# Reordering the token-major projections of a two-layer hybrid attention step, with their gates, rotations and inverse norms, its first loads and its end

## The chip, the core and the metric

The kernel runs on one core of a Trainium2 chip. The core has a matrix engine (TensorE, PE in the rows; PEld is its weight loads), VectorE (DVE), ScalarE (ACT), GpSimd (POOL) and a queue engine that issues most transfers (SyncE, SP). Each engine runs its own program in order; semaphores order work between engines. The metric is the device time of one execution: 3236.35 us, the median of three runs (3236.09 to 3236.82).

## The reference

Two post-norm layers over 128 context tokens and 512 latent tokens, width 1024. Each layer scales and shifts its input by a conditioning vector, projects it, mixes tokens in three head groups and projects back; then a dense feed-forward (first layer) or a top-2-of-8 expert feed-forward (second layer) follows, each with a residual and a layer norm.

```python
qa, ka, va, qkv_b, gate_b, a_b, b_b, qc, kc, vc = split_proj(h @ w_in_l)
oa = neighbourhood_attend(qa, ka, va, ...)
# gated DeltaNet, 4 heads, both directions
u = silu(short_conv(qkv, conv_w));  q, k, v = split(u, 3)
q = l2norm(q) * HEAD_DIM ** -0.5;   k = l2norm(k)          # x * rsqrt(sum(x*x) + 1e-6)
g = -exp(a_log) * softplus(a + dt_bias);  beta = sigmoid(b)
# differential attention: queries and keys of the latent tokens are rotated by their grid position
qc, kc = axial_rope(qc), axial_rope(kc)
x = layer_norm(ALPHA * x + g1 * (concat(oa, ob, oc) @ w_out))
x = layer_norm(ALPHA * x + g2 * channel_mixer(modulate(x)))
```

`a_b` and `b_b`, the decay and write gates, are 16 columns of the combined projection.

## The kernel before

The 640 tokens are five tiles of 128 (tile 0 is the context). A float32 product is done as three products of rounded words: a matrix is split in a rounded part ("high", cast by ScalarE) and the rest ("low", subtracted by VectorE), and high by high, high by low and low by high are summed. Weights come in loads of 1 MB through a ring of four slots; a load waits on `ring_used`, which TensorE counts up when it is done with a slot. All order is written by hand, in one program per engine (`build`, one block each).

**Start.** SyncE loads the conditioning, the constants and the five tiles of x (lines 617 to 622), then eight 1 MB blocks of the conditioning weights (line 628, from line 631). TensorE turns each block into six vectors per layer, block after block (`rows_of`, `columns_of`, lines 758 and 768), with ScalarE between (lines 1317, 1324). Then x is turned and modulated (lines 790 and 1743).

**Projections.** First 18 feature-major tiles (`FT`, line 819). Then 25 token-major groups n = 0 to 24 (`VT`, line 842): chunks c = 0 to 3 of 256 columns (values and output gates), five token tiles each, then c = 4, the 16 gate columns of five tiles. A group is 24 products, each with its own 128x128 weight load. VectorE empties the even groups (line 1801), ScalarE the odd ones (line 1368). Beside them VectorE runs six short convolutions (`convolve`, line 1786), one after each fourth group, and ScalarE their silu (line 1372).

**Between the projections and the DeltaNet.** After the last group, TensorE transposes the context keys for the output (line 852), multiplies the six rotated tiles by a permutation (line 858), sums squares of four tiles over each head (line 867), transposes keys and values (line 874) and sums the gates along time (lines 880, 882). GpSimd, VectorE: rotation (lines 2202, 1812, 1814). ScalarE: square, then log and exp for the inverse norm of one tile at a time (`square`, `inverse_norm`, lines 1387, 1394, 1397); VectorE multiplies by it (line 1828). ScalarE copies keys and values (line 1407), then softplus, exp of the gates (lines 1411 to 1419). Only then does the first of five DeltaNet units start (line 901).

**End.** The experts' rows are gathered by token (GpSimd, line 2180), scaled (ScalarE, line 1611), summed (VectorE, line 2140), multiplied by the gate row (GpSimd, line 2186); then residual and statistics of all five tiles (lines 2145, 2147), one inverse deviation for all (lines 1613, 1614), the two steps of the norm for all five (lines 2063, 2066), and five stores (lines 733, 735) behind one wait for all tiles.

## Time and profile before

| | |
|---|---|
| median of three runs | 3236.35 us |
| the profiled execution | 3239.69 us |
| its span in the trace | 3237.9 us |
| busy TensorE, VectorE, ScalarE, GpSimd | 2872.3, 1784.2, 1308.3, 338.0 us |
| share of the chain that ended last: TensorE, VectorE, ScalarE | 77%, 9%, 6% |

Times in rows are microseconds from the span's start unless marked ns. Of a row of the chain the columns are start, length, what. A matmul's length includes its way through the pipeline, so the spacing of starts, not the length, is what one of many costs. "Granted clock" is 1.00 for 2.4 GHz and 0.50 for 1.2 GHz. An idle time stands in brackets with what ended it.

### The profile page before, as it was taken

How to read it: one execution, taken by the hardware profiler on the slowest of the kernel's cores; microseconds unless marked ns; L12 is line 12 of the kernel's file. 1: busy time of each engine (PE TensorE's matmuls, PEld its weight loads, DVE VectorE, ACT ScalarE, POOL GpSimd, SP SyncE). 2: the span in 40 equal slices, each digit the busy share in tenths (PEclk: the TensorE clock that was granted, in tenths of full speed). 3: DMA queues.
4: the chain of work that ended last, by engine and by line, in shares of the span. 5: the costliest groups of instructions: out<-in, count | busy, mean ns of one | idle time of the engine just before them, and what ended most of it. 6: DMA issues, size and time to landing. Idle time of an engine off the chain costs nothing.

```text
span 3237.9 us, 51526 instructions
## 1 busy us (share of the span) xinstructions
PE 2872.3 (89%) x21532; PEld 2548.6 (79%) x21532; DVE 1784.2 (55%) x2706; ACT 1308.3 (40%) x1918; POOL 338.0 (10%) x335
## 2 busy tenths in 40 slices
PE   6997987897889999979979879988699999999992
PEld 5995776665889899769957766668589999899991
DVE  2243444667632222352524456666488888888886
ACT  2114222354132122131242224451477777777771
POOL 0002121100210000100021220002100000000002
PEclk9996988799999999979969888989899999999996
DMA  5251220000021221232221210003599999999992
GB/s 207 79 176 58 77 107 36 24 1 1 21 97 64 74 90 61 91 138 72 79 69 54 107 41 19 1 1 126 195 366 356 376 354 366 364 356 375 354 364 104
DMA packets 76518, 477.43 MB, mean 147 GB/s; under 512 B 10225, under 2 KB 13809, under 8 KB 26865
## 3 DMA queue, kind: packets, MB, share of 16 engines
q1 hardware_dynamic: 52672, 316.84, 26.1%
q0 software_dynamic: 23616, 157.30, 12.9%
q8 instruction: 173, 2.83, 0.3%
q14 instruction: 57, 0.46, 0.0%
HBM read 455.49 MB, written 27.53 MB: 149 GB/s over the span
## 4 chain that ended last, share of the span: by engine, by line
PE 77%; DVE 9%; ACT 6%; issue 4%; DMA 3%; POOL 1%; DVEq 0%; SPq 0%; ACTq 0%
PE psum L1258 14%; PE psum L1157 10%; PE psum L819 8%; PE psum L1280 7%; PE psum L842 5%; PE psum L1187 4%; PE psum L1118 4%; PE psum L1065 2%; DMA ring<-in_ada 2%; PE psum L931 2%; PE psum L1023 2%; PE psum L941 2%; ACT stage_rounded L1564 2%; PE psum L954 1%; PE psum L1050 1%
## 5 line engine op out<-in xcount | busy, mean ns | idle before, releaser
L1258 PE MATMUL psum<-stage_rounded 128*128 128x256 f32 x3728 | 571.6, 287 | 11.0 <-DVE ring_rounded L1633 4.3
L1258 PEld LDWEIGHTS psum<-stage_rounded 128*128 128x128 f32 x3728 | 512.7, 191 | 27.9 <-DVE ring_rounded L1633 11.8
L1633 DVE TENSOR_TENSOR ring_rounded<-ring,stage_rounded 128x2048 fp32r<-128x2048 f32 (+1 forms) x145 | 319.2, 2216 | 2.4 <-ACT stage_rounded L1564 2.4
L1633 DVE TENSOR_TENSOR stage_rounded<-stage,stage_rounded 128x2048 fp32r<-128x2048 f32 (+1 forms) x144 | 317.9, 2223 | 0.0
L1564 ACT CAST stage_rounded<-ring 128x2048 fp32r<-128x2048 f32 (+1 forms) x145 | 269.3, 1863 | 44.2 <-PE psum L1280 28.8
L1564 ACT CAST stage_rounded<-stage 128x2048 fp32r<-128x2048 f32 (+1 forms) x144 | 268.5, 1869 | 43.3 <-PE psum L1280 28.6
L1280 PE MATMUL psum<-stage_rounded 128*128 128x512 f32 x940 | 251.9, 394 | 0.1
L1459 ACT ACTIVATE stage<-psum,arena 128x640 f32<-128x640 f32 (+1 forms) x180 | 126.5, 706 | 231.5 <-DVE arena L1955 231.5
L1258 PE MATMUL psum<-ring_rounded,stage_rounded 128*128 128x256 f32 x760 | 215.3, 283 | 0.0
L1280 PEld LDWEIGHTS psum<-stage_rounded 128*128 128x128 f32 x940 | 175.1, 188 | 42.9 <-DVE stage_rounded L1633 3.7
L1065 PEld LDWEIGHTS psum<-stage 128*128 128x128 f32 x1008 | 135.0, 204 | 67.5 <-issue 35.7
L1065 PE MATMUL psum<-stage 128*128 128x128 f32 x1008 | 153.2, 299 | 29.3 <-ACT stage L1466 16.7
L1157 PE MATMUL psum<-stage_rounded 128*128 128x320 f32 x704 | 161.8, 311 | 12.0 <-POOL ring_rounded L2258 12.0
L1955 DVE TENSOR_REDUCE arena<-psum 128x1 f32<-128x640 f32 (+1 forms) x180 | 123.1, 712 | 73.9 <-PE psum L1026 38.2
L1157 PE MATMUL psum<-input_rounded,stage_rounded 128*128 128x320 f32 x704 | 161.5, 311 | 0.0
L1157 PE MATMUL psum<-stage_rounded,ring_rounded 128*128 128x320 f32 x704 | 161.1, 310 | 0.0
L1534 ACT CAST stage_rounded<-ring 128x2048 fp32r<-128x2048 f32 (+2 forms) x38 | 64.0, 1683 | 239.8 <-PE psum L1157 130.9
L1258 PEld LDWEIGHTS psum<-ring_rounded,stage_rounded 128*128 128x128 f32 x760 | 145.9, 192 | 0.3
L1435 ACT COPY stage<-psum 128x512 f32<-128x512 f32 x100 | 58.6, 586 | 210.5 <-PE psum L941 210.5
L1753 DVE TENSOR_TENSOR ring_rounded<-ring,stage_rounded 128x2048 fp32r<-128x2048 f32 x26 | 59.5, 2290 | 141.5 <-ACT stage_rounded L1344 141.5
L2117 DVE TENSOR_TENSOR stage<-stage,psum 128x640 f32<-128x640 f32 x22 | 18.1, 822 | 216.5 <-PE psum L1157 216.5
L1187 PE MATMUL psum<-stage_rounded 128*128 128x512 f32 x440 | 135.9, 389 | 0.0
(303 smaller groups left out, 6061.8 us busy)
## 6 DMA issues: line engine op xcount, KB each, us to landing
ring<-in_ada SPq DMA_DIRECT2D x48, 1024.0 KB, 4.9
ring<-in_moe_gu SPq DMA_DIRECT2D x48, 1024.0 KB, 7.3
ring<-in_moe_gu POOLq DMA_DIRECT2D x47, 1024.0 KB, 8.0
stage<-in_moe_gu SPq DMA_DIRECT2D x46, 1024.0 KB, 7.5
stage<-in_moe_gu POOLq DMA_DIRECT2D x46, 1024.0 KB, 7.6
ring<-in_unit SPq DMA_DIRECT2D x22, 1024.0 KB, 4.7
stage<-in_moe_down SPq DMA_DIRECT2D x22, 1024.0 KB, 7.4
stage<-in_moe_down POOLq DMA_DIRECT2D x22, 1024.0 KB, 7.8
```

The lines of the kernel that those rows point to most:

```text
L819: mm = pe.matmul(bank(b + g, 0, HALF), w[:, i % 2, k, :], r32(x[:, k, g * HALF:(g + 1) * HALF]), start=(k == 0 and m == 0), stop=(k == KD ...
L842: mm = pe.matmul(bank(b, 0, 256 if c < 4 else 16), r32(x[:, k, t * P:(t + 1) * P]), w[:, k, :], start=(k == 0 and m == 0), stop=(k == KD - ...
L1065: mm = pe.matmul(bank(7, 256, 256 + P), probT[j % 2][:, s * P:(s + 1) * P], VT[:, s, v_at:v_at + P], start=(s == 0), stop=(s == n - 1))
L1118: mm = pe.matmul(bank(n % 4, 0, 256), r32(x[:, k, t * P:(t + 1) * P]), w[:, k, :], start=(k == 0 and m == 0), stop=(k == KD - 1 and m == 2))
L1157: mm = pe.matmul(bank(b + 2 * i + g, 0, HALF), w[:, i, k, :], r32(x[:, k, g * HALF:(g + 1) * HALF]), start=(k == 0 and n == 0), stop=(k == ...
L1187: mm = pe.matmul(bank(b), r32(x[:, f, cols]), w[:, j, :], start=(f == 0 and m == 0), stop=(f == UF - 1 and m == 2))
L1258: mm = pe.matmul(bank(h % 2, 0, 2 * P), r32(x[:, cols]), w[:, k, :], start=(k == 0 and m == 0), stop=(k == KD - 1 and m == 2))
L1280: mm = pe.matmul(bank(4 + g), r32(x[:, f, :]), w[:, at], start=(f == 0 and m == 0), stop=(f == UF - 1 and m == 2))
L1459: act.activation(dst, src, ACT.Exp, bias=nb[:, s:s + 1], accum_out=sm[:, s:s + 1]).then_inc(a_exp, 1)
L1564: act.copy(r32(M_HIGH[q % M_HI][:, 0:n]), M_SLOT[q % M_SLOTS][:, 0:n]).then_inc(a_mhi, 1)
L1633: v.tensor_tensor(r32(w), w, high(M_HIGH[q % M_HI][:, 0:n]), ALU.subtract).then_inc(v_mlo, 1)
L1955: v.tensor_reduce(nb[:, s:s + 1], src, AX.XY if t else AX.X, ALU.max, negate=True).then_inc(v_nb, 1)
```

## The change

The 16 gate columns become the first five token-major groups (`TOKM_ORDER`), and their moving operand is repeated eight times, so that each of their 120 products has 128 columns (eight equal copies; only 16 are read). The gates' arithmetic on ScalarE and VectorE moves between the later groups (after n = 4, 7, 10, 16, 19 and 22), the gates' sums on TensorE after n = 13. The six rotation products follow groups 2, 6, 10, 14, 18, 22, all in PSUM bank 5, and VectorE's rotation follows every fourth group. Squares of three of the four tiles move into the loop. Behind the loop the sums of squares go in six pieces to six banks, ScalarE takes six logs and then two exps over two tiles each, the keys' first; the transposes wait for the keys alone. The silu of the output gates and the conditioning's silu come after the copies of keys and values. At the start the tiles of x are issued after the fourth conditioning block. At the end each tile's sum, residual, statistics, deviation, norm and store follow one another. The buffers of the moved values move with them: the rotation's product to `RL` with one buffer in place of two, the squares to the buffers that then hold the inverse norms.

```diff
+        SUM_BANKS = (4, 5, 1, 2, 3, 0)
+
+        def piece(p):
+            return (norm_k, norm_q)[p // 3][:, NORM_CUTS[p % 3]:NORM_CUTS[p % 3 + 1]]
...
-            for t in range(TILES):
-                sp.dma_start(xt[t], x_in[t * P:(t + 1) * P, :]).then_inc(s_x_in, 16)
...
                 for i in range(ADA_FIRST):
                     load(ada_in[l, i], i)
+                    if l == 0 and i == RING - 1:
+                        for t in range(TILES):
+                            sp.dma_start(xt[t], x_in[t * P:(t + 1) * P, :]).then_inc(s_x_in, 16)
...
-            sp.wait_ge(v_x2, mixed_before(DEPTH))
+            sp.wait_ge(v_x2, mixed_before(DEPTH - 1, 1))
             sp.dma_start(y_prompt, xt[0]).then_inc(s_y_out, 16)
             for t in range(1, TILES):
+                sp.wait_ge(v_x2, mixed_before(DEPTH - 1, t + 1))
                 sp.dma_start(y_sample[(t - 1) * P:t * P, :], xt[t]).then_inc(s_y_out, 16)
...
                 for n in range(25):
-                    c, t = n // TILES, n % TILES
+                    i, t = n // TILES, n % TILES
+                    c = TOKM_ORDER[i]
                     if t == 0:
-                        pe.wait_ge(v_pl, PROJ * l + FEAT_LOADS + c + 1)
+                        pe.wait_ge(v_pl, PROJ * l + FEAT_LOADS + i + 1)
...
-                            mm = pe.matmul(bank(b, 0, 256 if c < 4 else 16), r32(x[:, k, t * P:(t + 1) * P]), w[:, k, :],
+                            wk = w[:, k, :] if c < TOKM_LOADS else w[:, k, :].unsqueeze(1).broadcast_to([P, 8, 16])
+                            mm = pe.matmul(bank(b, 0, 256 if c < TOKM_LOADS else P), r32(x[:, k, t * P:(t + 1) * P]), wk,
                                            start=(k == 0 and m == 0), stop=(k == KD - 1 and m == 2))
-                            if k == 0 and t == 0 and m == 0:
+                            if k == 0 and t == 0 and m == 0 and i != 1:
                                 mm.then_inc(ring_used, 1)
...
+                    if n % 4 == 2:
+                        r = n // 4
+                        if r == 0:
+                            pe.wait_ge(s_rope, 16 * (l + 1))
+                        else:
+                            pe.wait_ge(v_rot, 12 * l + 2 * (r - 1) + 1)
+                        pe.matmul(bank(5), perm, FT[:, 12 + r, P:TOK], start=True, stop=True).then_inc(s_rot, 1)
...
+                        pe.wait_ge(v_g, l + 1)
...
+                        mm.then_inc(s_gc, 1)
...
+                def sum_squares(p):
+                    x = piece(p)
+                    pe.matmul(bank(SUM_BANKS[p], 0, x.shape[1]), blocks, x, start=True, stop=True).then_inc(s_ss, 1)
+
+                pe.wait_ge(a_sq, 4 * l + 3)
+                pe.wait_ge(v_gc, 2 * l + 1)
+                pe.wait_ge(v_rot, 12 * l + 11)
+                sum_squares(0)
+                sum_squares(1)
...
                 pe.wait_ge(a_tokm, 12 * l + 12)
                 for j, i in enumerate((3, 4, 5, 15, 16, 17)):
                     mm = pe.transpose(bank(6 + j // 4, (j % 4) * P, (j % 4 + 1) * P), FT[:, i, 0:P], ident)
+                    if j == 0:
+                        mm.then_inc(ring_used, 1)
                     if j in (3, 5):
                         mm.then_inc(s_kt, 1)
...
+                sum_squares(2)
+                pe.wait_ge(a_sq, 4 * l + 4)
+                for p in range(3, 6):
+                    sum_squares(p)
+
+                pe.wait_ge(v_norm, 4 * l + 2)
+                pe.wait_ge(a_silu, 6 * l + 6)
                 for t in range(TILES):
...
+                pe.wait_ge(a_kout, l + 1)
+                pe.wait_ge(v_kout, l + 1)
+                pe.wait_ge(v_norm, 4 * l + 4)
                 pe.wait_ge(a_kv, 5 * l + 5)
                 pe.wait_ge(v_gc, 2 * l + 2)
...
+                    if i == FEAT_TILES - 1:
+                        act.wait_ge(s_par, 16 * (l + 1))
+                        act.copy(r32(ab_hi), par[:, PR_WAB:PR_WAB + KD * 16]).then_inc(a_ph, 1)
                     projection_high(i // 2 + 1)
...
-                    if n in (1, 7, 11):
-                        projection_high(FEAT_LOADS + 1 + n // TILES)
-                    if n == 17:
-                        act.wait_ge(s_par, 16 * (l + 1))
-                        act.copy(r32(ab_hi), par[:, PR_WAB:PR_WAB + KD * 16]).then_inc(a_ph, 1)
+                    c, t = TOKM_ORDER[n // TILES], n % TILES
+                    if n in (1, 11, 17):
+                        projection_high(FEAT_LOADS + (1, 11, 17).index(n) + 1)
                     act.wait_ge(s_tokm, 25 * l + n + 1)
-                    w = 256 if c < 4 else 16
+                    w = 256 if c < TOKM_LOADS else 16
                     act.copy(VT[:, t, c * 256:c * 256 + w], bank([0, 1, 2, 3, 6, 7][n % 6], 0, w)).then_inc(a_tokm, 1)
...
+                        if i in (0, 2, 3):
+                            act.wait_ge(a_silu, 6 * l + i + 1)
+                            act.activation(norms[i], FT[:, 6 + i, :], ACT.Square).then_inc(a_sq, 1)
+                    if n == 7:
...
+                    if n == 19:
+                        act.wait_ge(v_gc, 2 * l + 2)
...
+                act.wait_ge(s_tokm, 25 * (l + 1))
+                act.activation(norms[1], FT[:, 7, :], ACT.Square).then_inc(a_sq, 1)
                 act.wait_ge(s_kt, 2 * l + 1)
+                act.copy(kout[:, 0:512], bank(6)).then_inc(a_kout, 1)
+
+                for p in range(6):
+                    x = piece(p)
+                    act.wait_ge(s_ss, 6 * l + p + 1)
+                    act.activation(x, bank(SUM_BANKS[p], 0, x.shape[1]), ACT.Ln, bias=RMS_EPS).then_inc(a_ln, 1)
+                act.wait_ge(a_ln, 6 * (l + 1))
+                for x in (norm_k, norm_q):
+                    act.activation(x, x, ACT.Exp, scale=-0.5).then_inc(a_rs, 1)
+
+                for t in range(TILES):
+                    act.wait_ge(s_kvt, 5 * l + t + 1)
+                    act.copy(KV[:, t, :], bank(t)).then_inc(a_kv, 1)
...
                 spread_cond()
-
                 act.wait_ge(v_tokm, 13 * l + 13)
                 act.wait_ge(a_tokm, 12 * l + 12)
                 act.activation(VT[:, :, 768:1024], VT[:, :, 768:1024], ACT.Silu).then_inc(a_gsil, 1)
...
+            def weigh(t):
                 act.wait_ge(s_gt[t], 32)
                 act.wait_ge(v_route, WEIGHED)
                 act.activation(YS[0][:, t, :], YS[0][:, t, :], ACT.Identity, scale=wts[:, 5 + t:6 + t]).then_inc(a_y, 1)
-            act.wait_ge(v_var, NORMS * DEPTH)
-            link(act.activation(rstd, mv.rearrange("p (t c) -> p t c", t=TILES)[:, :, 1], ACT.Ln, bias=LN_EPS))
-            act.activation(rstd, rstd, ACT.Exp, scale=-0.5).then_inc(a_rstd, 1)
+
+            def last_deviation(t):
+                act.wait_ge(v_var, NORMS * DEPTH - 1 + t + 1)
+                link(act.activation(rstd[:, t:t + 1], mv[:, 2 * t + 1:2 * t + 2], ACT.Ln, bias=LN_EPS))
+                act.activation(rstd[:, t:t + 1], rstd[:, t:t + 1], ACT.Exp, scale=-0.5).then_inc(a_rstd, 1)
+
+            for t in range(3):
+                weigh(t)
+            for t in range(TILES):
+                last_deviation(t)
+                if t + 3 < TILES:
+                    weigh(t + 3)
...
-                for n in range(0, 25, 2):
-                    c, t = n // TILES, n % TILES
-                    if n in (2, 6, 12):
-                        projection_low(FEAT_LOADS + 1 + n // TILES)
-                    if n == 18:
-                        v.wait_ge(a_ph, PROJ * (l + 1))
...
-                for r in range(6):
+                ab = VT[:, :, 1024:1040]
...
+                def rotate(r):
                     x = FT[:, 12 + r, P:TOK]
                     v.wait_ge(s_rot, 6 * l + r + 1)
                     v.wait_ge(g_rot, 6 * l + r + 1)
-                    v.tensor_tensor(x, bank(r), sinT, ALU.mult).then_inc(v_rot, 1)
+                    v.tensor_tensor(x, bank(5), sinT, ALU.mult).then_inc(v_rot, 1)
                     v.wait_ge(v_rot, 12 * l + 2 * r + 1)
-                    v.tensor_tensor(x, x, rot[:, (r % 2) * 512:(r % 2 + 1) * 512], ALU.add).then_inc(v_rot, 1)
-
...
+                for n in range(0, 25, 2):
+                    c, t = TOKM_ORDER[n // TILES], n % TILES
+                    if n in (2, 12, 18):
+                        projection_low(FEAT_LOADS + (2, 12, 18).index(n) + 1)
...
+                    if n == 4:
...
+                    if n % 4 == 0 and n < 24:
+                        convolve(n // 4)
+                    if n == 10:
+                        v.wait_ge(a_gate, 6 * l + 3)
...
+                    if n == 16:
+                        v.wait_ge(s_gc, l + 1)
+                        v.tensor_copy(gct, bank(4, 0, 80)).then_inc(v_gc, 1)
...
+                    if n == 22:
+                        v.wait_ge(a_gate, 6 * (l + 1))
...
+                    if n % 4 == 0 and n:
+                        rotate(n // 4 - 1)
+
+                v.wait_ge(s_kt, 2 * l + 2)
+                v.tensor_copy(kout[:, 512:768], bank(7, 0, 256)).then_inc(v_kout, 1)
...
+                for j in (2, 3, 0, 1):
                     x = FT[:, 6 + j, :]
-                    v.wait_ge(a_rs, 4 * l + j + 1)
-                    v.scalar_tensor_tensor(x, x, HD ** -0.5 if j < 2 else 1.0, norms[j % 2], ALU.mult, ALU.mult).then_inc(v_norm, 1)
...
+                    v.wait_ge(a_rs, 2 * l + (1 if j >= 2 else 2))
+                    v.scalar_tensor_tensor(x, x, HD ** -0.5 if j < 2 else 1.0, norms[j], ALU.mult, ALU.mult).then_inc(v_norm, 1)
...
+
+                    def residual(t):
+                        v.wait_ge(g_xg, TILES * l + t + 1)
+                        link(v.scalar_tensor_tensor(xt[t], xt[t], ALPHA, YS[1][:, t, :], ALU.mult, ALU.add))
+                        for i in range(2):
+                            link(v.bn_stats(st_m[:, 12 * t + 6 * i:12 * t + 6 * i + 6], xt[t][:, i * 512:(i + 1) * 512]))
+                        carry(v)
+                        v.bn_aggr(mv[:, 2 * t:2 * t + 2], st_m[:, 12 * t:12 * t + 12]).then_inc(v_var, 1)
+
+                    def last_norm(t):
+                        v.wait_ge(v_var, NORMS * DEPTH - 1 + t + 1)
+                        link(v.scalar_tensor_tensor(xt[t], xt[t], mv[:, 2 * t:2 * t + 1], ln_g, ALU.subtract, ALU.mult))
+                        v.wait_ge(a_rstd, NORMS * DEPTH - 1 + t + 1)
+                        v.scalar_tensor_tensor(xt[t], xt[t], rstd[:, t:t + 1], ln_b, ALU.mult, ALU.add).then_inc(v_x2, 1)
+
+                    combine_rows(0)
+                    combine_rows(1)
+                    residual(0)
+                    combine_rows(2)
+                    for t in range(1, TILES):
+                        residual(t)
+                        if t + 2 < TILES:
+                            combine_rows(t + 2)
+                        last_norm(t - 1)
+                    last_norm(TILES - 1)
...
-
-                pool.wait_ge(s_tokm, 25 * (l + 1))
                 for r in range(6):
                     i = 12 + r
                     pool.wait_ge(a_feat if i % 2 else v_feat, 9 * l + i // 2 + 1)
-                    if r >= 2:
-                        pool.wait_ge(v_rot, 12 * l + 2 * (r - 1))
-                    pool.tensor_tensor(rot[:, (r % 2) * 512:(r % 2 + 1) * 512], FT[:, i, P:TOK], cosT, ALU.mult).then_inc(g_rot, 1)
+                    if r:
+                        pool.wait_ge(v_rot, 12 * l + 2 * r)
+                    pool.tensor_tensor(rot, FT[:, i, P:TOK], cosT, ALU.mult).then_inc(g_rot, 1)
```

On TensorE, at the end of the token-major groups of the first layer, before:

```order
L842 MATMUL psum<-stage_rounded 128x16 x2
L842 MATMUL psum<-stage_rounded,input_rounded 128x16
L852 MATMUL psum<-arena,stage 128x128 x6
L858 MATMUL psum<-stage 128x512 x6
L867 MATMUL psum<-stage,arena 128x320 x8
L874 MATMUL psum<-arena,stage 128x128 x20
L880 MATMUL psum<-arena 128x20 x2
L882 MATMUL psum<-arena 128x20 x2
L901 MATMUL psum<-stage 128x128 x2
```

and at the same place of the changed program, where L858 is the token-major product, L880 a sum of squares, L891 the context keys, L905 keys and values and L926 the first DeltaNet unit:

```order
L858 MATMUL psum<-stage_rounded 128x256
L858 MATMUL psum<-stage_rounded,input_rounded 128x256
L880 MATMUL psum<-arena 128x512 x2
L891 MATMUL psum<-arena,stage 128x128 x6
L880 MATMUL psum<-arena 128x256
L880 MATMUL psum<-stage,arena 128x512 x2
L880 MATMUL psum<-stage,arena 128x256
L905 MATMUL psum<-arena,stage 128x128 x20
L926 MATMUL psum<-stage 128x128 x2
```

The 16-column groups, the six rotation products and the four gate sums are gone from this place (they stand earlier), and the eight sums of squares are six.

On ScalarE, in the same stretch, before (L1387 square, L1394 log, L1397 exp; ACT_TABLE_LOAD switches the function table):

```order
L1387 ACTIVATE stage<-stage 128x640 x2
L1394 ACT_TABLE_LOAD
L1394 ACTIVATE stage<-psum 128x640
L1397 ACT_TABLE_LOAD
L1397 ACTIVATE stage<-stage 128x640
L1387 ACTIVATE stage<-stage 128x640
```

a pattern that runs four times. In the changed program, from the last square to the copies of keys and values:

```order
L1416 ACTIVATE stage<-stage 128x640
L1418 COPY stage<-psum 128x512
L1423 ACT_TABLE_LOAD
L1423 ACTIVATE arena<-psum 128x512 x2
L1423 ACTIVATE arena<-psum 128x256
L1423 ACTIVATE stage<-psum 128x512 x2
L1423 ACTIVATE stage<-psum 128x256
L1426 ACT_TABLE_LOAD
L1426 ACTIVATE arena<-arena 128x1280
L1426 ACTIVATE stage<-stage 128x1280
L1430 COPY stage<-psum 128x512 x5
```

Eight table loads between the squares and the copies have become two.

On VectorE, at the very end, the changed program has for one tile after the other (L2181 residual, L2183 and L2185 statistics, L2176 sum of the next tile's rows, L2189 and L2191 norm of the tile before):

```order
L2181 SCALAR_TENSOR_TENSOR arena<-arena,stage 128x1024
L2183 BN_STATS stage<-arena 128x6 x2
L576 MEMSET arena 128x1
L2185 BN_AGGR arena<-stage 128x2
L2176 SCALAR_TENSOR_TENSOR stage<-stage,arena 128x1024
L2189 SCALAR_TENSOR_TENSOR arena<-arena 128x1024
L2191 SCALAR_TENSOR_TENSOR arena<-arena 128x1024
```

where before each of these steps ran over all five tiles before the next.

## Rows read from the trace of the kernel before

**Rows 1.** Windows: busy time by engine with counts, granted clock, DMA share, GB/s.

```profile
184.60:241.70 57.10, 57.05 (x480) 57.08 (x481) 33.89 (x59) 11.62 (x17) 0.00 (x0) 1.00 0.68 231
247.20:262.50 15.30, 15.27 (x73) 15.18 (x72) 2.38 (x6) 0.98 (x3) 0.00 (x0) 0.50 0.00 1
264.07:271.00 6.93, 6.93 (x13) 2.95 (x13) 5.01 (x7) 4.41 (x6) 3.59 (x3) 0.74 0.63 189
```

**Rows 2.** The chain that ended last, both layers: start, length, what.

```profile
184.65 77.83 PE psum L842 x600
264.28 6.89 PE psum L858 x12
288.51 0.84 DVE stage L1828
289.39 4.54 PE psum L874 x20
301.30 1.19 PE psum L901 x4
...
1553.40 77.83 PE psum L842 x600
1670.04 1.19 PE psum L901 x4
```

**Rows 3.** Timeline of TensorE, the 16-column groups: start, length, instruction.

```profile
244.04 0.37 PE L842 MATMUL psum<-stage_rounded 128*128 128x16 f32 x2
244.38 0.37 PE L842 MATMUL psum<-stage_rounded 128*128 128x16 f32 x2
```

**Rows 4.** Timeline of TensorE, every fifth transpose of the input.

```profile
47.84 0.42 PE L791 MATMUL psum<-arena 128*128 128x128 f32 x1
...
48.91 0.42 PE L791 MATMUL psum<-arena 128*128 128x128 f32 x1
...
49.60 0.27 PE L791 MATMUL psum<-arena 128*128 128x128 f32 x1
...
50.15 0.27 PE L791 MATMUL psum<-arena 128*128 128x128 f32 x1
```

**Rows 5.** Timeline of TensorE behind the projections; unrounded products are two instructions each.

```profile
262.74 1.54 PE L852 MATMUL psum<-arena,stage 128*128 128x128 f32 x6 [0.27 <-DVE stage L1801]
...
271.00 1.24 PE L867 MATMUL psum<-stage,arena 128*128 128x320 f32 x4
...
280.40 2.50 PE L867 MATMUL psum<-stage,arena 128*128 128x320 f32 x4 [2.39 <-ACT stage L1387]
...
298.67 1.04 PE L880 MATMUL psum<-arena 128*128 128x20 f32 x4 [4.75 <-DVE arena L1833]
```

**Rows 6.** Timeline of ScalarE behind the projections.

```profile
264.69 1.26 ACT L1381 ACTIVATE stage<-stage 128x1280 f32<-128x1280 f32 x1
...
275.68 1.28 ACT L1394 ACT_TABLE_LOAD   x1
276.97 0.70 ACT L1394 ACTIVATE stage<-psum 128x640 f32<-128x640 f32 x1
...
293.95 0.59 ACT L1407 COPY stage<-psum 128x512 f32<-128x512 f32 x1 [0.27 <-PE psum L874]
```

**Rows 7.** Timeline of VectorE, a convolution's taps and the rotation's sum.

```profile
233.76 0.55 DVE L1781 TENSOR_SCALAR arena<-stage,arena 128x640 f32<-128x640 f32 x1
234.34 4.28 DVE L1786 SCALAR_TENSOR_TENSOR arena<-stage,arena 128x126 f32<-128x126 f32 x8
...
239.13 0.42 DVE L1801 COPY stage<-psum 128x256 f32<-128x256 f32 x1 [0.30 <-PE psum L842]
...
266.75 0.69 DVE L1814 TENSOR_TENSOR stage<-stage 128x512 f32<-128x512 f32 x1
...
272.00 1.32 DVE L1814 TENSOR_TENSOR stage<-stage 128x512 f32<-128x512 f32 x1
```

**Rows 8.** The chain, at the start.

```profile
6.10 12.16 DMA ring<-in_ada
...
20.79 4.73 DMA ring<-in_ada
```

**Rows 9.** Windows, at the start.

```profile
16.00:18.00 2.00, 1.84 (x16) 0.56 (x15) 0.00 (x0) 0.03 (x1) 0.00 (x0) 1.00 1.03 434
```

**Rows 10.** Timeline of VectorE, GpSimd and SyncE, the end.

```profile
3191.48 8.77 DVE L2140 SCALAR_TENSOR_TENSOR stage<-stage,arena 128x1024 f32<-128x1024 f32 x3 [1.25 <-ACT stage L1611]
...
3223.61 6.07 DVE L2066 SCALAR_TENSOR_TENSOR arena<-arena 128x1024 f32<-128x1024 f32 x5
...
3191.07 3.96 POOL L2186 TENSOR_TENSOR stage<-stage,arena 128x1024 f32<-128x1024 f32 x2
...
3230.10 3.73 SPq L735 DMA_DIRECT2D out_y_sample<-arena  x4
```

**Rows 11.** DMA issues: KB each, median us from issue to landing.

```profile
out_y_prompt<-arena SPq DMA_DIRECT2D x1, 512.0 KB, 2.7
```

163 lines of the change are left out of this document (60 added, 103 removed).

## The prediction

> **What bounds the kernel now.** I read the chain that ended last first, then windows over the two stretches that the change touches most, then timelines engine by engine. The chain is 77% TensorE. In each layer it goes through the token-major stage, 77.83 us for 600 products, and from its end to the start of the first DeltaNet unit through a stretch in which engines wait for each other in turn: 184.65 + 77.83 = 262.48 to 301.30 is 38.8 us [rows 2]. The second layer has the same numbers: 1670.04 − 1553.40 = 116.6, as 301.30 − 184.65. So a token-major stage with what follows is 116.6 us, twice, and what it loses or gains is the program's, since TensorE is waited for by all that follows.
>
> In the stage the 480 products of 256 columns keep TensorE busy 57.05 us at granted clock 1.00, the upper level (2.4 GHz): 0.119 each, 2.85 for a group of 24. The other 120, of 16 columns, take the rest, 77.8 − 57.05 = 20.8 us [rows 1, 2]. They begin at 0.34 per three, 0.113 each [rows 3], so the 128x128 weight load and not the columns sets their pace; from 247.2 on the clock stands at 0.50, the lower level (1.2 GHz), and they cost 15.27 / 73 = 0.209 [rows 1].
>
> In the stretch behind, TensorE is mostly waiting. Six rotation products take 6.89 at a mean clock of 0.74; then come four rounds of square, table load (1.28), log (0.70), table load, exp, one tile each; one multiplication on VectorE (0.84); 20 transposes (4.54), a copy behind each four (0.59); and 6.8 us of gates: softplus, two table loads, sums of gates, from 293.95 + 0.59 to 301.30 [rows 2, 5, 6].
>
> **The token-major stage, part by part.** *Gate groups.* 120 products of 128 columns at the front. The nearest row for a product with its own 128x128 weights and 128 columns is a transpose of the input: five take 1.07 at the lower level and 0.55 at the upper, 0.214 and 0.110 [rows 4]. Half the columns of the other products, so the weight load is again the limit, and I take the 0.113 of 16 columns: 120 x 0.113 = 13.6 instead of 20.8, −7.2. Bounds: 0.110 and 0.25 (rivals).
>
> *Rotation products.* Six of 512 columns between groups. Behind the projections they start 1.15 apart at clock 0.74 (6.89 / 6), so 0.85 at 1.00; I take 0.9, +5.4. *Gate sums*, after n = 13: two pairs, each 1.04 at the lower level [rows 5], half of it at the upper, +1.0. *Waits.* Each group needs a bank emptied six groups before, and the rotation products share one bank that VectorE has to empty. A convolution of eight taps holds VectorE 0.55 + 4.28 = 4.8 us [rows 7], under two groups (5.7), so the six banks nearly cover it; with the rotation's sum (0.69 to 1.32, six times) queued behind it I put 1.5 us of stall on TensorE, 0 to 6. The stage ends at 57.05 + 13.6 + 5.4 + 1.0 + 1.5 = 78.6 us, 0.8 later than now.
>
> The Trainium skill (GPSIMD Engine Reference, the specifications of section 1) says that GpSimd shares its SBUF interfaces with VectorE and contends with DVE instructions of two SBUF inputs; that speaks against laying the rotation, half of which is GpSimd's, beside the convolutions. The trace has the same sum on VectorE at 0.69 and at 1.32 [rows 7], so six sums could cost 3.8 us of VectorE more, but it has slack between groups; by that rule the stall would be nearer its upper bound.
>
> *What becomes hidden.* Gates on ScalarE and VectorE, three of four squares and the silu of the output gates (1.26, now ahead of the first square [rows 6]) leave the path. ScalarE was busy 11.62 of 57.10 us beside the products and VectorE 33.89 [rows 1]; table loads of softplus and exp (1.28 each) fit there. If that cover were gone, ScalarE's evictions of odd groups would come late, by 1.28 to 2.6 us once or twice: this is in the 0 to 6.
>
> **The stretch behind, after the change.** In the order in which one waits for the other: last eviction (0.42) and last rotation sum (0.69) with hand-over, 1.15; two sums of squares over 512 columns at 0.9, 1.8; six transposes that now stand between (first start to the next line's, 264.07 − 262.74 = 1.33; 1.2 taken); copy for the output 0.6; one table load 1.28; logs of 2560 columns at 0.70 per 640, 2.8 + 0.1; one table load 1.28; exp of the keys' two tiles, 1280 columns, 1.26; two multiplications on VectorE, 1.68; 20 transposes 4.54; last copy 0.6 [rows 2, 5 to 7]. Sum 18.2 us against 38.8, −20.6. Late next is the log and exp chain on ScalarE, then the transposes, which still go one after the other with their copies. The queries' multiplications (1.68) and their exp lie beside the transposes. The gates' softplus and exp are done long before. The 18.2 could be 16 (transposes at the upper level) or 23 (lower level throughout, contention on VectorE).
>
> Per layer −20.6 + 0.8 = −19.8, both −39.6.
>
> **The start.** The first two conditioning blocks' transfers share the wire with x now: the second lands 12.16 us after its issue, a later one 4.73 [rows 8]. With x behind the fourth block the early ones come up to 5 us sooner. But x, 2.6 MB, at 434 GB/s [rows 9] takes 6 us, and then stands before the fifth block, so the last block, for which the modulation waits, comes no earlier. I take 0; bounds −3 (part of the gain survives) and +2 (x itself late for the transposes).
>
> **The end.** VectorE does the same work tile by tile: its last norm steps are 6.07 for five [rows 10], and the first tiles' stores leave while later tiles are worked on. Now one store and four more follow one another in the queue, from 3229.70 to 3230.10 + 3.73 = 3233.83, and the end is at 3237.9, 8.2 us after the last norm. After the change one store of 512 KB remains: 0.35 of issue and 2.7 to land [rows 11], 3.1 us; −5.1. On the other side VectorE now waits at each tile for ScalarE's deviation, and GpSimd's multiplication (1.98 each of two) is in step with it: sums beside GpSimd take 2.9 each (8.77 for three) [rows 10]. For this I put +1.5 (0 to +5). Net −3.5, from −6 to 0.
>
> Other moves cost nothing that is on the path: the third conditioning load of the second block is issued by SyncE at the key transposes, ahead of the DeltaNet's loads and stores, and its weights are used only after the projections that follow; the conditioning's silu, with one table load, moves behind the key and value copies, where TensorE has its first unit to do. If one of them held the unit, the price is 1.28 per layer.
>
> **Sum.** −39.6 + 0 − 3.5 = −43.1. The profiled execution is 3239.69 (span 3237.9), 3.3 above the median of 3236.35, so 3196.6 on its scale and 3193 on the median's.
>
> **Rivals.**
> *The wide products run as unrounded ones.* They have 128 columns and a repeated operand; no row of before shows a rounded product of fewer than 256 columns at speed except at 16. Unrounded 512-column products cost 1.15 at clock 0.74, 0.85 at 1.00, so 0.21 per 128; two of 320 columns take 1.24, 0.62 each, 0.25 per 128, with the way through the pipeline in it [rows 5]. At 0.225 the gate groups are 27.0, +13.4 per layer against my sum, 3220. For it: nothing above but that the price of 16 columns hides any number of passes. Against: the operands are marked rounded as in all 256-column products. The Trainium skill (FP8 and Floating Point Precision, TensorE Precision Notes) has reduced-precision fp32 read in four bytes and cut, and true fp32 in four passes through the array; four passes of 53 ns (128 columns at 2.4 GHz, an estimate) are 0.21, which agrees with the rows above. Chance 0.12.
>
> *The clock falls beside the gate groups anyway,* as it did after 5 us of 16 columns [rows 1, 3]. Against: during the transposes of 128 columns it rose to the upper level, with other work between [rows 4], and the engine comes from 320-column products. At 0.209 each, 120 cost 25.1, +11.5; I charge the lower level for about two thirds of them as now, +7.2, and 1.7 for the first groups behind at the lower level: +8.9 per layer, 3211. Chance 0.12.
>
> *Slower than before: both together.* Unrounded passes at the lower level: two of 320 columns take 2.50 there [rows 5], 0.50 per 128, 60 us of gate groups, +46 per layer, 3286. It decides from 13.6 + 21.5 = 35.1 us per stage, 0.29 per product, where the whole gain is gone. Against the lower level: that 2.50 was taken after TensorE had stood idle for 2.39, and the gate groups follow on other products without a pause. Chance 0.04.
>
> *Nothing arrives:* TensorE reaches the DeltaNet 20 us earlier and there waits for a transfer. Against: the wire is idle before it (DMA share 0.00, [rows 1]) and SyncE's next loads are released by TensorE itself. About 3230 to 3240; chance 0.04.
>
> **How the numbers follow.** My forecast has 0.68, its own range 3186 to 3204: each stage's stall (0 to 6 each, so −3 to +9 on two), the start (−3 to +2) and the end (−2.5 to +3.5) rarely at one side together. The range to 3184 below and 3221 above takes in the clock rival and most of the first, and leaves about 0.15 out. Two-tenths of a per cent, 6.5 us, is what a measurement can tell from no change: all but the last two rivals are faster by more than that, 0.93 with part of the fourth; same 0.03; slower 0.04.
>
> **What would show it.** The 128-column products' starts 0.113 apart at clock 1.00 (0.21 to 0.25 at 1.00: first rival; 0.21 at 0.50: second); the first unit about 97 us after the first token-major product in both layers; two table loads between squares and copies; waits of the rotation products for VectorE of 1 to 2 us in all; the span's end 3 us after the last norm. Wrong would be a stage over 82 us, or a stretch over 23 us behind it.

## The result and the profile after

The changed kernel takes 3182.39 us (the median of 3181.69, 3181.80, 3182.98 and one disturbed execution of 11222.7 us, which the ratio leaves out) against 3236.59 us beside it: a ratio of 0.9827, 95% interval 0.9813 to 0.9840. That is 54.2 us less. The forecast was 3193, range 3184 to 3221: the direction was right, the time lies 1.6 us below the range, and the gain was under-estimated by 11 us.

The profiled execution has a span of 3180.0 us. First the stages by windows (columns as in rows 1: window, length, busy time of TensorE, its weight loads, VectorE, ScalarE and GpSimd with counts, granted clock, DMA share, GB/s). The changed kernel, first layer: gate groups, the sums of squares with the wait for logs and exps, the key and value transposes, the opening of the first DeltaNet unit (its first products, until the conditioning's rows begin):

```profile
183.10:191.20 8.10, 8.06 (x72) 8.09 (x73) 4.98 (x11) 2.07 (x2) 0.00 (x0) 1.00 0.38 131
263.40:274.60 11.20, 5.20 (x18) 2.80 (x18) 2.65 (x5) 8.20 (x11) 0.00 (x0) 0.92 0.64 208
274.66:279.20 4.54, 4.53 (x20) 4.13 (x20) 1.42 (x2) 2.34 (x4) 0.00 (x0) 0.50 0.01 5
280.07:285.50 5.43, 5.43 (x50) 4.95 (x50) 0.69 (x1) 4.43 (x5) 0.00 (x0) 1.00 0.01 3
```

and of the kernel before the two that answer to the last two, which the forecast did not look at as a pair:

```profile
289.39:293.90 4.51, 4.51 (x20) 4.12 (x20) 0.00 (x0) 2.34 (x4) 0.00 (x0) 0.50 0.00 0
301.30:311.40 10.10, 10.10 (x52) 9.20 (x56) 0.96 (x3) 1.63 (x5) 2.26 (x2) 0.50 0.01 2
```

The gate groups hold the upper level; the same products that open the first unit take 10 us at 0.50 before and 5.4 us at 1.00 now. That is the large thing that the forecast lacked. What TensorE did ahead of the unit, by its first products (the bracket is the idle time before them, and what ended it) and by windows in its waits, before:

```profile
301.30 1.19 PE L901 MATMUL psum<-stage 64*128 64x128 f32 x4 [0.73 <-DVE arena L1840]
294.00:298.60 4.60, 0.00 (x0) 0.00 (x0) 0.39 (x3) 4.05 (x8) 0.00 (x0) 0.50 0.00 0
```

and in the changed kernel, the wait for logs and exps early and late, and the wait behind the transposes:

```profile
268.70:272.50 3.80, 0.00 (x0) 0.00 (x0) 0.00 (x0) 3.77 (x7) 0.00 (x0) 1.00 0.89 276
273.00:274.60 1.60, 0.00 (x0) 0.00 (x0) 1.56 (x3) 1.17 (x2) 0.00 (x0) 0.50 0.75 277
279.75:280.05 0.30, 0.00 (x0) 0.01 (x1) 0.00 (x0) 0.28 (x2) 0.00 (x0) 1.00 0.00 0
280.07 0.68 PE L926 MATMUL psum<-stage 64*128 64x128 f32 x4 [0.88 <-ACT stage L1430]
```

In both kernels the transposes run at 0.50, behind a long wait. In the changed one the level comes back in the 0.88 us behind them; before, it stays at 0.50 through the 4.75 us, the gate sums and the opening. The 4.6 us do arrive: from the unit's first product to the second load's conditioning rows it was 17.9 us (301.30 to 319.21) and is 13.2 (280.07 to 293.28).

The chain of the changed kernel has the stage in pieces, with the rotation products between (start, length, what), and the second layer like the first:

```profile
183.14 8.23 PE psum L858 x72
191.36 0.91 PE psum L869 x2
192.27 5.32 PE psum L858 x48
...
274.66 4.54 PE psum L905 x20
...
1527.88 8.23 PE psum L858 x72
...
1619.42 4.54 PE psum L905 x20
```

The first 72 products take 8.23 us, 0.114 each. From the first to the last product it is 183.14 to 262.29, 79.15 us [before 77.83, rows 2]. Behind them the chain of the changed kernel goes through these pieces:

```profile
262.65 0.69 DVE stage L1828
263.35 0.14 issue
263.48 1.96 PE psum L880 x4
265.44 0.45 PE psum L891 x4
265.89 0.02 issue
265.91 0.58 ACT stage L1418
266.50 0.02 issue
266.51 1.28 ACT L1423
267.80 0.01 issue
267.81 1.36 ACT arena L1423 x3
269.17 1.25 ACT stage L1423 x3
270.43 0.02 issue
270.44 1.28 ACT L1426
271.73 0.01 issue
271.74 1.28 ACT arena L1426
273.02 0.02 issue
273.04 1.57 DVE stage L1874 x2
```

Rotation's end, sums, transposes of the context keys, output copy, table load, logs, table load, one exp, two multiplications: one after the other as the forecast had them, and the transposes (274.66) and copies behind. The first unit starts at 280.07: 17.8 us behind the last product, where it was 38.8.

The end, VectorE and SyncE of the changed kernel (start, length, instruction):

```profile
3134.31 1.28 DVE L2176 SCALAR_TENSOR_TENSOR stage<-stage,arena 128x1024 f32<-128x1024 f32 x1 [17.37 <-ACT stage L1628]
...
3141.62 3.01 DVE L2181 SCALAR_TENSOR_TENSOR arena<-arena,stage 128x1024 f32<-128x1024 f32 x1 [2.88 <-POOL stage L2239]
...
3163.84 13.47 SPq L748 DMA_DIRECT2D out_y_sample<-arena  x4
...
3175.66 1.28 DVE L2191 SCALAR_TENSOR_TENSOR arena<-arena 128x1024 f32<-128x1024 f32 x1
```

The last norm ends at 3176.94, the span 3.1 us later; before it was 8.2 [rows 10]. From the first sum to the last norm VectorE takes 42.6 us, before 44.1 (3185.59 to 3229.68).

Where the 57.9 us between the spans (3237.9 and 3180.0) come from, by starts in both traces:

| stretch | before | after | difference |
|---|---|---|---|
| up to the first feature product | 55.26 | 55.28 | 0.0 |
| token-major stage, layer 1 | 77.83 | 79.15 | +1.3 |
| from there to the first unit, layer 1 | 38.8 | 17.8 | −21.0 |
| these two together, layer 2 (1553.40 to 1670.04; 1527.88 to 1624.83) | 116.64 | 96.95 | −19.7 |
| opening of the first unit, twice (both layers alike) | 10.02 each | 5.42 each | −9.2 |
| end, from TensorE's last product | 63.8 | 58.4 | −5.4 |
| the rest (feature products of the first layer 1.5, DeltaNet units) | | | −3.9 |

The rest is not the change's: a second profile of the kernel before (below) differs from the first by as much in the same stretches, and the profiled execution of before lay 3.3 us above its median. Without it, 39.4 + 9.2 + 5.4 = 54.0, beside the 54.2 that were measured.

### The profile page after: what moved, and what is told of

Read it like the earlier page. It is cut to its first block, busy times and chain, and to the rows that moved or that the text cites. A ratio compares the mean times of both kernels' runs of the same rounds, so it can differ in the third digit from the quotient of the medians.

```text
span 3180.0 us, 51506 instructions
## 1 busy us (share of the span) xinstructions
PE 2834.8 (89%) x21524; PEld 2516.3 (79%) x21524; DVE 1780.5 (56%) x2706; ACT 1319.6 (41%) x1934; POOL 341.3 (11%) x335
## 4 chain that ended last, share of the span: by engine, by line
PE 76%; DVE 10%; ACT 5%; issue 4%; DMA 3%; POOL 1%; DVEq 0%; SPq 0%; ACTq 0%
PE psum L1283 15%; PE psum L1182 10%; PE psum L832 8%; PE psum L1305 8%; PE psum L1212 4%; PE psum L1143 4%; PE psum L858 3%; PE psum L1090 3%; DMA ring<-in_ada 2%; PE psum L956 2%; PE psum L1048 2%; PE psum L966 2%; ACT stage_rounded L1581 2%; PE psum L979 2%; PE psum L771 1%
## 5 line engine op out<-in xcount | busy, mean ns | idle before, releaser
L2126 DVE TENSOR_TENSOR ring_rounded<-ring,stage_rounded 128x2048 fp32r<-128x2048 f32 (+2 forms) x36 | 71.9, 1996 | 115.7 <-ACT stage_rounded L1551 115.7
```

## The experiments

Theory A: TensorE stands idle just before the first unit and so opens it at the lower level; the change took the gates' chain out of that place, and with it the idle time. Rival B: the level follows from the changed order of the stage before, or comes and goes by chance. Rival C, which came up on the way: narrow products count like idle time. The runs were made in three sets, in which the kernel before took 3238.66, 3238.64 and 3240.12 us where it took 3236.59 beside the changed kernel above; so the ratios, and not the times, are to be compared across sets.

**The kernel before, unchanged.**

> The kernel before, unchanged, for a second profile. Its profiled execution was 3239.69 us where the median was 3236.4. Theory A (the difference is the clock of single stretches in that one execution): a second profile has another total by 1 to 4 us, and the stretches in which it differs show another granted clock, while the opening of the first DeltaNet unit (10.0 us from its first product to the conditioning rows, clock 0.50) is the same in both layers. Rival: the opening itself varies from execution to execution; then it is not 10.0 us here, and the 9.2 us that it lost in the changed kernel are chance.

3235.2 us in its one execution, span 3233.5. The openings are 9.87 and 10.02 us. The stretch from the second layer's last conditioning load in the chain to the output norm at line 2002 (1832.30 to 2163.59) is 331.3 us, in the first profile 333.8 (1833.45 to 2167.23); the feature products of the first layer end 1.7 us sooner (182.91 for 184.65), and the way from there to the key and value transposes takes 1.6 more. So single stretches vary by some us, the opening of before does not. The level ahead of it does: in the first layer it came back behind the transposes (1.00 from 294.00 to 297.00) and was down again from 297.50 on, before the wait of 4.75 us was over; in the other three openings of before it did not come back at all.

**A pause put back into the changed kernel.**

```diff
                 for t in range(TILES):
                     act.wait_ge(s_kvt, 5 * l + t + 1)
+                    if t == TILES - 1:
+                        for _ in range(10):
+                            link(act.copy(KV[:, t, :], bank(t)))
                     act.copy(KV[:, t, :], bank(t)).then_inc(a_kv, 1)
```

> The changed kernel, with ten more copies of the same bank on ScalarE ahead of the last copy of keys and values, 6 to 7 us in each layer for which TensorE waits between the transposes and the first unit; the order is not changed otherwise. Theory A (idle time just before the unit sets its clock): besides the 6 to 7 us the opening goes back from 5.4 to 10.0 us at clock 0.50, together +11 per layer and about 3204. Rival B (the clock there follows from the changed order of the stage before): the opening stays at 5.4, +6.5 per layer and about 3195.

3204.48 us, ratio to before 0.9892 (0.9875 to 0.9910): theory A's number. TensorE, first layer (the bracket is the idle time before, and what ended it), then the windows of the opening in both layers:

```profile
286.61 1.19 PE L926 MATMUL psum<-stage 64*128 64x128 f32 x4 [7.06 <-ACT stage L1433]
```

```profile
286.61:296.60 9.99, 9.99 (x48) 9.12 (x48) 0.69 (x1) 5.16 (x6) 1.35 (x2) 0.50 0.01 2
1641.95:1651.90 9.95, 9.95 (x48) 9.12 (x48) 0.69 (x1) 5.16 (x6) 1.31 (x2) 0.50 0.01 2
```

Nothing was moved, 6.2 us of idle time were added (7.06 for 0.88), and the opening is 10 us at 0.50 again. In the second layer the level can be watched in the wait, in which TensorE does nothing:

```profile
1636.00:1639.00 3.00, 0.00 (x0) 0.00 (x0) 0.00 (x0) 2.84 (x6) 0.00 (x0) 1.00 0.00 0
1639.50:1641.90 2.40, 0.00 (x0) 0.00 (x0) 0.00 (x0) 2.29 (x5) 0.00 (x0) 0.50 0.00 0
```

It came back behind the transposes and fell within the pause. In the first layer it did not come back before the unit was open (0.50 up to 297.5). So the pause acts in two ways, and both end in a slow opening: six of six openings behind a long wait took 9.9 to 10.0 us.

**The gap of the kernel before filled.** Six, nine, and nine and two unread products:

```diff
+                for _ in range(6):   # 9 in the second and third
+                    pe.matmul(bank(7, 256, 512), ident, keep[:, 0:256], start=True, stop=True)
                 pe.wait_ge(v_g, l + 1)
...
+                for _ in range(2):   # in the third alone
+                    pe.matmul(bank(7, 256, 512), ident, keep[:, 0:256], start=True, stop=True)
                 pe.wait_ge(a_kv, 5 * l + 5)
```

> The kernel before, with six products whose results nobody reads (256 columns, unrounded) put on TensorE between the key and value transposes and the gate sums, where TensorE stands idle for 4.75 us. Nothing else is moved. Theory A (the first unit opens at the lower clock because TensorE stands idle just before it): the opening falls from 10.0 to about 5.4 us at clock 1.00, the gate sums from 1.9 to about 1, so about -5 per layer and 3226 in all. Rival B (the opening is fast in the changed kernel for what was moved ahead of it, or for ScalarE's and VectorE's other work, and not for TensorE's idle time): the opening stays at 10.0 us and the time at 3236 to 3237, or some us more if the products overrun the gap.

> The kernel before with nine unread products in place of the six of the run before, so that less of the 4.75 us gap stays idle. With six, 1.3 to 1.6 us of idle time were left ahead of the gate sums and 0.73 behind them; the opening began at clock 1.00 and fell back to 0.50 for part of it (7.0 us in the first layer, 8.9 in the second). Theory A (idle time before and between decides): with three more the opening is 5.4 us in both layers, and the stretch from the first key transpose to the conditioning rows falls from 21.9 to about 17, -5 per layer, 3226 to 3228. Rival B: the openings stay as with six, as they do not follow the idle time, 3233.

> The kernel before with nine unread products ahead of the gate sums, as in the run before, and two more behind them, in the 0.73 us for which TensorE waits there. What stays between the transposes and the first unit is 0.3 to 0.5 us of idle time and the 20-column gate sums. Theory A (idle time on TensorE, however short, brings the lower level back): the opening is 5.4 us at 1.00 in both layers, as there is less idle time than the 0.88 us of the changed kernel; about -5 per layer. Rival C (narrow products count like idle time, as the 16-column groups at the front did): the opening begins at 1.00 and falls back as it did with nine, 8.9 to 9.2 us, and the time stays within 2 us of before.

Six: ratio 0.9984 (0.9975 to 0.9994), openings 7.0 and 8.9 us. Nine: 0.9998 (0.9988 to 1.0008), 9.2 and 9.0 us. Both began the unit at the upper level and fell back within it, so the first two did not give what theory A promised, and nine gave no more than six. With the last 0.73 us filled too, windows of the opening in both layers:

```profile
301.17:306.60 5.43, 5.43 (x49) 4.97 (x48) 0.96 (x3) 1.48 (x4) 0.34 (x1) 1.00 0.00 0
1665.94:1671.40 5.46, 5.46 (x51) 4.98 (x50) 0.96 (x3) 1.48 (x4) 0.38 (x1) 1.00 0.00 0
```

Time 3229.26, ratio 0.9966 (0.9953 to 0.9979): 11 us gained (7 to 15 by the interval), without moving one instruction of the kernel. So the clock term exists by itself, and it is had without the changed order: that half of rival B falls; what is left of chance shows below. How much of the gap has to be filled was not as simple as I had it.

**Narrow products in the changed kernel's wait.**

```diff
+                for d in range(4):
+                    pe.matmul(bank(7, 256 + 20 * d, 276 + 20 * d), ones, g3[:, :, 4 * (d % 2):4 * (d % 2) + 4], start=True, stop=True)
                 pe.wait_ge(v_norm, 4 * l + 4)
                 pe.wait_ge(a_kv, 5 * l + 5)
```

> The changed kernel with four unread products of 20 columns (two instructions each, as the gate sums) behind the key and value transposes, in the 0.88 us for which TensorE waits there anyway; their operands are the gates. Theory A: no change of the opening, 5.4 us in both layers, and about 0.5 us per layer for what of them overruns the wait. Rival C (narrow products count like idle time and what decides is how much of a stretch they and idle time take together): the opening falls back to 0.50 for part of it, 7 to 9 us, +2 to +4 per layer.

3183.42 us, openings 5.46 us in both layers. A few narrow products in place of the wait do not keep the level from coming back; rival C falls at this size.

**16 columns in place of 128, still in front.**

```diff
-   wk = w[:, k, :] if c < TOKM_LOADS else w[:, k, :].unsqueeze(1).broadcast_to([P, 8, 16])
+   wk = w[:, k, :]
```

> The changed kernel, with 16 columns in place of 128 in the gate groups, which stay at the front. My forecast's working took 0.113 us per product at 128 columns and clock 1.00, and saw the width as what keeps the clock. Theory W (width): the first groups run at 0.113, then the clock falls to 0.50 as it did at the back, 0.209 each; the five groups take 18 to 22 us in place of 13.6, the first groups behind them some of it at 0.50; +6 to +9 per layer, 3195 to 3200. Rival P (place: at the front, behind 320-column products, the clock holds): 13.6 us as with 128, no change.

3208.89 us, ratio 0.9911 (0.9894 to 0.9927): 26.0 us above the run with x last, below, which is of the same set and as fast as the changed kernel. Windows of the front of the stage:

```profile
183.60:189.10 5.50, 5.46 (x41) 5.49 (x41) 2.53 (x6) 1.90 (x1) 0.00 (x0) 0.81 0.57 194
189.10:210.00 20.90, 20.90 (x93) 19.87 (x94) 6.42 (x13) 1.72 (x4) 0.00 (x0) 0.50 0.00 0
210.00:230.00 20.00, 19.80 (x152) 18.64 (x152) 13.09 (x26) 8.23 (x13) 2.56 (x2) 0.98 0.22 81
```

The place does not keep the clock, the width does. And the price is larger than both my forecast's 8.9 per layer and the 6 to 9 expected here, 10.6 in the first layer's stage (from its first product, 183.65, to the sums of squares, 274.63, it is 90.98 us for 80.34). The level falls at about 187.5, so nearly three quarters of the narrow products run at the lower one, where the forecast had two thirds; the rotation product among them takes 1.91 for 0.91; and the lower level stays on behind the last narrow product (207.85) until about 211. The two layers make 21 of the 26 us; the rest lies in the DeltaNet units, which vary. The opening of the first unit is 5.42 us here too, so a stage with a slow front does not slow it.

**x behind all eight conditioning blocks.**

```diff
-                    if l == 0 and i == RING - 1:
+                    if l == 0 and i == ADA_FIRST - 1:
```

> The changed kernel, with the loads of x behind all eight conditioning blocks of the first layer in place of behind the fourth. In the changed kernel the fifth block's rows wait 6.0 us for their load, as x (2.6 MB) lies ahead of it, and the first feature product starts at 55.28, 0.02 later than before. Theory A (x is only in the way of the fifth block): the fifth to eighth blocks come every 3.4 to 4 us, the transposes of x start at 41 in place of 45.9, the first feature product at about 50.5; -4 to -5 in all. Rival (x is then itself what is late, 2.6 MB behind 3 MB of conditioning at some 430 GB/s): start of the feature products within 1 us of 55.3.

3182.92 us; the first feature product starts at 55.01. The blocks did come sooner, but ScalarE then waited for the first feature weights:

```profile
48.01 1.90 ACT L1369 CAST stage_rounded<-ring 128x2048 fp32r<-128x2048 f32 x1 [7.66 <-DMA ring<-in_feat]
```

The rival's number for another reason: not x, but what is issued behind it is late. In the changed kernel the same place is the fifth block, TensorE:

```profile
29.25 1.93 PE L771 MATMUL psum<-ring,stage 128*32 128x256 f32 x16 [6.04 <-DMA ring<-in_ada]
...
55.28 0.56 PE L832 MATMUL psum<-stage_rounded 128*128 128x320 f32 x2 [1.00 <-DVE input L1769]
```

Three orders of the same loads, 55.26, 55.28 and 55.01: the wait moves, its end does not. The other profiles, with the first two of these orders, lie between 53.8 and 56.7, so 0.3 us tells nothing, but the gain of 4 to 5 that I expected would have shown.

**One wait for all stores.**

```diff
-            sp.wait_ge(v_x2, mixed_before(DEPTH - 1, 1))
+            sp.wait_ge(v_x2, mixed_before(DEPTH))
```

> The changed kernel, with all five stores behind one wait for all tiles, as in the kernel before; the order of the arithmetic at the end stays the changed one. It tells the two parts of the end apart: by my working the single last store is worth 5.1 us of the gain there and the order of the arithmetic costs 1.5. Theory: the span's end comes 8.2 us after the last norm in place of 3.1, about 3187 to 3188, and the arithmetic's length does not change. Rival (stores beside the arithmetic slow it, or the tail is set by something else): less than 3 or more than 7 us.

The span ends at 3188.7, the last norm at 3180.38, the stores in between:

```profile
3179.10 1.28 DVE L2191 SCALAR_TENSOR_TENSOR arena<-arena 128x1024 f32<-128x1024 f32 x1
3180.41 0.35 SPq L745 DMA_DIRECT2D out_y_prompt<-arena  x1
3180.80 3.73 SPq L748 DMA_DIRECT2D out_y_sample<-arena  x4
```

8.3 us behind the last norm in place of 3.1: the 5.1 of the working. The arithmetic takes 42.5 us here, with no store beside it (3137.85 to 3180.38), and 42.6 with four: the stores beside it cost it nothing. The median, 3189.62, is 7.2 above the changed kernel's; in this set the kernel before is 2.0 above its time there as well.

**The wait for logs and exps filled, and copies split.**

```diff
                 for p in range(3, 6):
                     sum_squares(p)
+                pe.wait_ge(v_kout, l + 1)
+                for _ in range(12):
+                    pe.matmul(bank(7, 256, 512), ident, keep[:, 0:256], start=True, stop=True)
...
-                for t in range(TILES):      # ScalarE; second experiment only
+                for t in (0, 2, 4):
...
+                for t in (1, 3):            # VectorE, behind its multiplications
+                    v.wait_ge(s_kvt, 5 * l + t + 1)
+                    v.tensor_copy(KV[:, t, :], bank(t)).then_inc(a_kv, 1)
```

> The changed kernel, with twelve products whose results nobody reads (256 columns, unrounded) on TensorE behind the sums of squares, while ScalarE takes logs and exps (about 6 us without work for TensorE, after which the 20 transposes ran at clock 0.50 in 4.54 us). Theory A: the transposes run at clock 1.00 and what they take is then set by ScalarE's copies (0.58 each, five of them): the stretch from the first transpose to the first unit falls from 5.4 to about 3.8, -1.6 per layer, 3179. Rival B (the clock does not follow TensorE's idle time): no change, 3182, or slower where the products overrun the gap.

> The changed kernel with the twelve unread products behind the sums of squares (the transposes then ran at clock 1.00 in 2.40 us and what followed was ScalarE's copies), and with the copies of tiles 1 and 3 on VectorE in place of ScalarE. Theory: from the first transpose to the first unit 3.6 us become about 3.0, the opening stays at 5.4 and 1.00; together 2.3 us per layer less than the changed kernel, 3177 to 3178 where that has 3182. Rival (VectorE's two copies come behind the queries' multiplications and are late): 3.6 us or more, and no gain over the fill alone.

With the fill the 20 transposes take 2.40 us at 1.00, and the first unit comes 3.65 and 3.52 us after the first of them (before the fill 5.41); with split copies 3.28 in both layers, openings 5.4. The window of the transposes with fill and split copies:

```profile
274.69:277.90 3.21, 2.40 (x20) 2.16 (x20) 2.69 (x4) 1.93 (x4) 0.00 (x0) 1.00 0.00 0
```

Times: 3180.48 with the fill (ratio 0.9810, 0.9793 to 0.9826), 3182.14 with both (0.9823, 0.9810 to 0.9837; five executions from 3177.82 to 3184.45). The stretch shortened as expected with the fill (3.8) and less than expected with both (3.0); the 3177 to 3178 expected for both were missed, and whether the split adds anything to the fill the times do not tell.

**The changed kernel again, on the chip of the last.**

> The changed kernel, unchanged, beside the run with filled gap and split copies on one chip. In all profiles so far the stretch of four DeltaNet units between the conditioning loads differed by up to 4 us from one execution to the next at the same program, so single totals tell less than the stretches. Expected: openings of 5.4 us in both layers, first transposes to first unit 5.4, and a median 3 to 5 us above the filled and split kernel. If the median is within 1 us of it, the fill's gain of 1.75 us per layer is given back behind.

3186.60 us (3185.56 to 3187.92), ratio 0.9835 (0.9821 to 0.9848): 4.5 above the filled and split kernel by the medians, with intervals that overlap; by the ratio this run is the changed kernel of above again (0.9835 for 0.9827). And the profile holds a surprise, windows of the opening in both layers:

```profile
279.66:289.60 9.94, 9.94 (x48) 9.12 (x48) 0.69 (x1) 5.17 (x6) 1.30 (x2) 0.50 0.01 2
1631.98:1637.40 5.42, 5.42 (x48) 4.94 (x48) 0.69 (x1) 4.42 (x5) 0.00 (x0) 1.00 0.01 3
```

The first layer's opening was slow here, with the same 0.88 us of idle time ahead of it as in the second. Of ten openings of the changed order with that wait as it is (five profiles: this one, the first, 16 columns, x last, one wait) nine took 5.4 us and this one 10.0. In all ten the level had fallen to 0.50 in the wait for logs and exps; nine times it came back at the end of the transposes or in the 0.88 us behind them, and here at about 293.5, long after the unit had opened. So taking the pause away gives the fast opening most of the time, not always.

The Trainium skill (TensorE: Matmul & The Clock Gate, Part 1) puts the fall of the clock on idle time, and says that the gate's look at TensorE does not start with the kernel, so that the same kernel can change level at another point in another run. The second layer of the run with the pause agrees with the first (the level fell within 7.05 us of waiting), this profile with the second. The forecast did not weigh that rule.

## Why the prediction was wrong, step by step

**The stage.** Gate groups: 120 products at 0.114 us and clock 1.00, as forecast (0.113). Rotation products wait 1.4 us for VectorE in all, four times, the longest 0.6; 1.5 was the term. 79.15 us against 78.6. The rotation's sums on VectorE were not lengthened: six at a mean of 692 ns, the shorter of the two lengths of rows 7. That is no test of the rule that the forecast took from the Trainium skill (GPSIMD Engine Reference, section 1): with one buffer in place of two each product of GpSimd starts when the sum before it is done (203.74 + 0.69, then 204.57), so the two never run together. Before, a sum took 1.32 us where such a product ran beside it (272.00, product from 271.51 to 272.78) and 0.69 where none did (266.75), which agrees with the rule.

**The stretch behind.** 17.8 us against 18.2, with two table loads and each piece within 0.3, but for the context keys' transposes, 0.45 on the chain for 1.2, of which the last copy with its hand-over (0.87 for 0.6) and the sums (1.96 for 1.8) give some back. Both parts together −19.7 per layer against −19.8; that they agree to 0.1 is luck, that they agree to 1 is not.

**The step that failed** is the sum's end point: "Per layer −20.6 + 0.8 = −19.8, both −39.6." It stops at the first product of the first unit and takes the unit as before. What it put at nothing was in the trace: TensorE idle for 4.75 us ahead of the gate sums [rows 5] and 0.73 behind them, in the very 6.8 us that the working called "6.8 us of gates", and the unit behind them at 0.50. Taking those away changes not only when the unit starts but at which clock: 10.02 to 5.42 us, 9.2 for both layers. I had asked what the clock does inside the moved groups (the second rival), and not what it does in the unchanged work behind the pause that goes. The pause put back, and the gap of before filled, showed the term by itself.

**The end.** −3.5 was −5.4. The last store was right (8.2 to 3.1, and back to 8.3 with one wait). The arithmetic was forecast 1.5 longer and became 1.5 shorter: three of VectorE's instructions beside GpSimd take 2.9 to 3.0 us now, before four did [rows 10, and 3.02 at 3200.18]; no run shows that this is the whole of it. The first sum starts 1.2 later behind TensorE's last product, since the store ahead of the gather landed in 3.90 us for 2.62. That is this execution's and not the change's: in seven of the nine profiles with the changed order the store landed in 2.6, so the end is worth nearer 6 us, and the 54.0 above is so close to 54.2 by some luck.

**The start.** 0, as forecast (55.28 for 55.26).

**The rivals.** Unrounded passes: no, 0.114 per product. Clock falling beside the gate groups: no, 1.00; but with 16 columns it falls in front as at the back, and costs more than I had put (10.6 for 8.9 per layer). The slower case needed both and did not come. Nor did TensorE wait for a transfer ahead of the unit: its 0.88 us there end with ScalarE's last copy. With the clock term the sum would have been 43.1 + 9.2 = 52.3 and the forecast 3184; the range to 3184 had no room below because none of its terms reached into the unit.

## What to carry to other kernels

When a change takes a pause out of TensorE's way, price the work behind the pause at both clock levels, as far as the trace shows the lower one: here that was a sixth of the gain, and it lay in code that the diff does not touch. Where the pause cannot go, unread products in it can buy the same (11 us here with eleven of them per layer), but only once the gap is filled to its end; half-filled ones gave 0 to 5. An order of loads at the start is worth looking at by its last landing: three orders moved the wait from one engine to another and not its end.

## What was not expected of the hardware

Filling nine products' worth of the gap gave no faster openings (9.2 and 9.0 us) than six (7.0 and 8.9), though it left less idle time (0.48 and 0.33 us ahead of the sums, for 1.33 and 1.62); all four started at 1.00 and fell back some products later, while TensorE was at work. And behind the same transposes and the same 0.88 us the level had come back nine times and once had not. Why the one and not the other is open; no run here tells it. The DeltaNet units vary by some us: 2.5 between the two profiles of before, and from 481.6 to 485.2 us over the profiles of before and its filled versions (from the first conditioning load in the chain behind the first unit to the output norm), so a change of 2 us in this kernel shows in the trace and not in a few totals.
